# First expert layer: when the rows scattered to DRAM are asked back, what waits behind them, and when they are added

## The reference

```python
y = jnp.zeros((B * S, D), jnp.float32)
for e in range(N_EXPERTS):
    hdn = jax.nn.silu(xt @ w_gate[e]) * (xt @ w_up[e])
    y = y + combine[:, e:e + 1] * (hdn @ w_down[e]).astype(jnp.float32)
...
h = h + g2[:, None, :] * grouped_moe(xn, router_w, router_b, moe_w_gate[layer],
                                     moe_w_up[layer], moe_w_down[layer])
```

## Time and profile before

| | us |
|---|---|
| median of 3 runs | 889.63 (889.59 to 893.86) |
| the profiled execution, its own time | 888.99 |
| its span, first to last instruction | 887.2 |
| PE busy | 844.6 (95%) |
| DVE busy | 329.3 (37%) |
| DMA, mean rate over the span | 358 GB/s |
| stretch of the change: end of layer 0's experts and start of the latent attention | about 469 to 550 |

### The profile page before, as it was taken

The page is one execution under the profiler, slowest core; times in us unless marked ns, Lnnn a source line. Parts: engine busy times, 40 slices in busy tenths (PEclk is TensorE's granted clock), DMA queues, the critical chain, the costliest instruction groups (busy, mean ns, idle before and its releaser), DMA issues.

```text
span 887.2 us, 11840 instructions
## 1 busy us (share of the span) xinstructions
PE 844.6 (95%) x4369; PEld 468.0 (53%) x4369; DVE 329.3 (37%) x598; ACT 177.3 (20%) x354; POOL 161.6 (18%) x271
## 2 busy tenths in 40 slices
PE   6999999999999899999999779999899999999996
PEld 4787444444444555545545347784555555545552
DVE  2826766955302322111112066768511112211114
ACT  2100112121102222122121141250322122122112
POOL 0024000000004522122210131400642212012111
PEclk9999999999999999999999899999999999999999
DMA  8999999998579599999999995579899999979994
GB/s 318 387 321 376 368 366 341 340 382 345 205 271 371 211 406 422 421 422 421 422 422 420 372 400 222 192 293 422 326 360 422 420 421 421 388 312 422 420 404 131
DMA packets 70014, 317.29 MB, mean 358 GB/s; under 512 B 10039, under 2 KB 10170, under 8 KB 44366
## 3 DMA queue, kind: packets, MB, share of 16 engines
q1 hardware_dynamic: 61594, 304.42, 85.6%
q0 software_dynamic: 4976, 8.40, 3.1%
q10 hardware_dynamic: 3396, 3.80, 1.3%
HBM read 311.31 MB, written 15.20 MB: 368 GB/s over the span
## 4 chain that ended last, share of the span: by engine, by line
PE 83%; DMA 6%; SPq 4%; DVE 3%; issue 2%; ACT 1%; ACTq 0%; POOL 0%; DVEq 0%; POOLq 0%
PE bank L730 12%; PE bank L912 11%; PE bank L930 11%; PE bank L899 10%; PE bank L771 6%; PE bank L874 6%; PE bank L671 5%; SPq L470 4%; PE bank L1127 3%; DMA acc<-in_moe_w_up 3%; PE bank L723 2%; DMA part<-outs 1%; PE bank L1081 1%; PE bank L922 1%; PE bank L554 1%
## 5 line engine op out<-in xcount | busy, mean ns | idle before, releaser
L1787 DVE TENSOR_TENSOR arena<-bank,arena 128x256 f32<-128x256 f32 x34 | 21.0, 617 | 254.4 <-PE bank L912 254.4
L1536 DVE SCALAR_TENSOR_TENSOR part<-ring,cpad,part 128x1024 f32<-128x1024 f32 x84 | 111.1, 1323 | 4.1 <-DMA ring<-in_w_mod 1.2
L730 PE MATMUL bank<-ring,xnT 128*128 128x512 f32 x256 | 111.2, 592 | 0.0
L899 PE MATMUL bank<-ring,arena 128*64 128x512 f32 x416 | 92.1, 595 | 0.0
L930 PE MATMUL bank<-ring,arena 128*64 128x512 f32 x352 | 81.7, 606 | 4.4 <-issue 4.4
L912 PE MATMUL bank<-ring,arena 128*64 128x256 f32 x704 | 80.3, 381 | 0.2 <-DMA ring<-in_moe_w_up 0.2
L730 PEld LDWEIGHTS bank<-ring,xnT 128*128 128x128 f32 x256 | 48.4, 190 | 59.4 <-issue 59.3
L874 PEld LDWEIGHTS bank<-arena,y 128*128 128x128 f32 x544 | 64.6, 198 | 15.2 <-issue 15.1
L874 PE MATMUL bank<-arena,y 128*128 128x128 f32 x544 | 67.5, 284 | 1.2 <-DVE arena L1747 1.2
L912 PEld LDWEIGHTS bank<-ring,arena 128*64 128x64 f32 x704 | 50.2, 137 | 30.2 <-issue 8.6
L1315 ACT ACTIVATE arena<-bank,modc,scale 128x128 f32<-128x128 f32 x68 | 25.7, 458 | 180.7 <-PE bank L874 180.7
(11 more groups left out here) (342 smaller groups left out, 1073.0 us busy)
## 6 DMA issues: line engine op xcount, KB each, us to landing
ring<-in_w_mod SPq DMA_DIRECT2D x48, 1024.0 KB, 12.6
ring<-in_moe_w_gate SPq DMA_DIRECT2D x48, 1024.0 KB, 15.4
ring<-in_moe_w_down SPq DMA_DIRECT2D x44, 1024.0 KB, 12.8
ring<-in_moe_w_up SPq DMA_DIRECT2D x40, 1024.0 KB, 12.6
ring<-in_ret_w_in SPq DMA_DIRECT2D x24, 1024.0 KB, 7.3
arena<-in_moe_w_down SPq DMA_DIRECT2D x12, 1024.0 KB, 17.0
arena<-in_moe_w_up SPq DMA_DIRECT2D x12, 1024.0 KB, 16.7
arena<-in_moe_w_gate SPq DMA_DIRECT2D x9, 1024.0 KB, 12.2
```

What stands on the lines that cost most here:

```text
L730: ins = pe.matmul(pair[tt][:], xnT[:, k, tok(tt)], w[:, k, :], start=(k == 0), stop=(k == KT - 1))
L899: ins = pe.matmul(bank[0][e * 64:(e + 1) * 64, :], xgT[:, k, e * 64:(e + 1) * 64], w(e, k), start=(k == 0), stop=(k == KT - 1))
L1536: ins = dve.scalar_tensor_tensor(o, w[:, k, :], c, o, ALU.mult, ALU.add)
```

## The change

It has three parts, all for layer 0 alone. POOL waits, ahead of the two DMAs that bring the rows back, until half 0 of down matrices 46 and 47 is in. SP waits for both of these DMAs to have landed before it issues the first latent weight. DVE adds `part` to `h` behind the two scalings of the last round instead of ahead of them. Layer 1 keeps its order.

```diff
@@ sync
                 if l == 0:
+                    sp.wait_ge(back_in, 32)
                     for j, (kind, n) in enumerate(MLA_ITEMS):
@@ vector, round_of(u, last)
-                    if last:
+                    def returned():
+
                         dve.wait_ge(back_in, 32 * (l + 1))
                         dve.scalar_tensor_tensor(h[:], part[:], first_time[:], h[:], ALU.mult, ALU.add).then_inc(S["h_added"], 1)
                         dve.wait_ge(S["h_added"], u * 6 + 4)
                         dve.memset(first_time[:], 0.0).then_inc(S["h_added"], 1)
+
+                    if last and l:
+                        returned()
                     dve.wait_ge(S["info_ready"], u + 1)
...
                     if last:
+                        if l == 0:
+                            returned()
                         into_h(u)
@@ gpsimd, experts(l)
                 pool.wait_ge(row_none, l + 1)
+                if l == 0:
+                    for m in (6 * PAIRS - 2, 6 * PAIRS - 1):
+                        b, k = HOMES[0][m]
+                        pool.wait_ge(landed[0][b] if b < RING else outside_in[0][b - RING], 16 * k)
                 back = outs[l].rearrange("(t p f) n -> p f t n", p=P, f=2)
```

## The result

The change made the kernel slower: 893.73 us in the median of 13 runs (890.13 to 896.07) beside 890.93 for the kernel before (13 runs); ratio 1.0026, 95% interval 1.0014 to 1.0038, about 2.3 us (the two medians lie 2.8 us apart). The forecast was 887.4, the range ended at 891.4. The three runs shown of before had a median of 889.63, so 1.3 us of the distance are the base; the sign was wrong all the same. The profiled execution took 891.49 us, its span is 889.7.

A forecast was written before the change was run, and what follows sets the result against it. The prediction took PE's waits in layer 0's experts, with rows taking bandwidth from down weights, as the bound. `into_h` 3.5 us earlier, less 1.3 us given back to mod 21, made -2.2 us: median 887.4, range 885.2 to 891.4.

The forecast's parts named there:

- The first PE wait: PE's 4.03 us idle before 494.28, until layer 0's last up weights are in; claimed to stay, with its slow stretch.
- the 4.36 us: PE's idle time before 512.79, until the last half of the down weights lands; claimed to go, with its slow stretch.
- The wait in SP: Step on the latent and mod 20/21 loads issued at 513.1 into an empty queue; claimed 1.3 us given back.
- 2 us of lost flow: Transfer time taken as lost when SP's queue restarts empty at 513.1, moving mod 21's landing from 536.4 to 538.4.
- the head start: 1.28 MB of latent and mod loads already through by 513 in the kernel before; its loss was put at nothing.
- I take 538.4: Forecast landing of mod 21's second half, 536.4 before, with only the 2 us lost.
- the argument on the slowest engine: Claim that the slowest DMA engines, which set a landing, had done next to nothing of the latents at 513.0.
- The prediction's other end, 541.4: Landing of mod 21's second half if all of the 1.28 MB already moved by 513 before is lost.
- the slower rival: Latents and mods start too late, PE waits 4.9 us for mod 21: 890.4, or 892.4 with a slow stretch; chance 0.2.
- PE's clock falls in the new gap: Rival: PE waits 2.8 us for the normalised rows behind its filler and its clock drops: 888.1; chance 0.2.
- The rows come later: Rival: the returned rows land at 515 instead of 513.1, `into_h` starts at 517.6: 889.6, no gain; chance 0.1.
- does not do what it says: Rival: the last down half lands as before because the rows were not what held it: 892; chance 0.03.

The follow-up runs named there:

- sp_only: The kernel before with SP's wait for the returned rows alone added; ratio to before 0.9990.
- mods_first: The changed kernel with SP loading mod 20 and 21 ahead of qa, kvb and qb; ratio to before 0.9973.
- no_move: The changed kernel with the addition of `part` back ahead of the scalings; ratio to before 1.0002.
- warm: The changed kernel with five filler matmuls ahead of PE's waits for mod 21 and the rope products; ratio to before 1.0006.
- mods_early: The changed kernel with SP waiting for the first row DMA alone and loading mod 20 and 21 right behind kva; ratio to before 0.9959.
- early_hold: The changed kernel with a semaphore for each row DMA, SP waiting for the first alone; ratio to before 0.9981.
- early_warm: The changed kernel with SP waiting for the first row DMA alone and five instead of three fillers behind PE's products; ratio to before 0.9972.
- move_only: The kernel before with the addition of `part` moved behind the scalings and nothing else; ratio to before 1.0061.

## Why the prediction was wrong

**Right, to half a us.** The first PE wait stays. The last down half arrives in time, the 4.36 us and the slow stretch behind them go. The rows land at the same time as before. The addition lands on the path and costs 2.5 of the 6 us that PE gains. `into_h` starts at 515.65 (forecast 515.7), kva's loads are issued at 513.2, and PE does not wait for kva. POOL's copy of kva was to stay at 526.55 and came at 528.45, behind the landing of the scatter of no rows; it held PE's rope matmuls (L1006 of before) back by 0.9 us.

**The step that failed** is in "The wait in SP": "I take 2 us of lost flow", with the head start put at nothing, and from it "I take 538.4". It was 542.06, 5.2 us later than before by T, where 2.0 were forecast; sp_only measures the same term by itself: 4.9 us. From SP's release to mod 21 the loads took 28.8 us (513.22 to 542.06), and 27.5 to 28.6 in the five other kernels with a hold and the old order of loads, where the kernel before needed 23.7 from its last down half (512.7 to 536.42).

What the runs show of the reason is the following. The total of the bytes fits: 1.3 MB less up to the release and 0.9 MB less in the 7.3 us behind it make 5.1 us. The flow came back slower than was taken: 229, 310, 351 and 367 GB/s in the four stretches of 2 us from 514 on. But the argument on the slowest engine was not what failed. A load counts its semaphore up 16 times, at times that the trace holds, and it has landed with the last of these counts. In the kernel before, the counts of the last down half came from 502.6 to 512.7, and the last ones of kva's halves followed at 513.8 and 514.8: what was last had indeed done nothing of the latents at 512.7, although kva's first counts came at 508.2. It went on at the full rate, to 536.3 for mod 21 (8.65 MB and ACT's 1.05 MB in 23.6 us are 0.41 MB/us); in the changed kernel the last count came at 542.0. The spread had shrunk from 10.1 us to 3.1 by then (533.2 to 536.3), so whoever was ahead lost most of that lead again. The prediction's other end, 541.4 (541.8 by T), thus had the number, "if all of the head start is lost"; how the 5.2 us divide into head start and restart is not shown and stays open. The row that the choice had to be weighed by (7.37 of 8.65 MB) stood in the text.

**What followed from it** was the slower rival, chance 0.2, "890.4 without that, 892.4 with it": L613 at 548.65, an idle stretch of 5.0 us (forecast for that case 4.9) and the slow clock behind it. Its 892.4 is 2.8 us above the base of then: the distance of the two medians, and 0.5 us more than the ratio gives. Two things have to be kept apart. Why nothing was gained: the late mod 21 took all that `into_h` had won, and mods_first, where it is out of the way, is 4.7 us faster than the changed kernel. Why there was a loss: with the late mod 21 but no slow stretch behind it, no_move and warm are level with before, 2.1 and 1.8 us better than the changed kernel. So nearly all of the 2.3 us are the clock behind PE's wait. From the intervals each of the two differences is uncertain by nearly its own size (an estimate: 1.8 and 1.7 us). What carries the reading is that both agree, and that in both traces the four matmuls took 1.9 to 2.0 us instead of 3.75.

**The rivals.** "PE's clock falls in the new gap" was not what the profile after shows (1.9 us idle, clock 1.00), but mods_first and mods_early show that case, with 1.5 to 2.9 us on kva's matmuls. The Trainium skill (TensorE: Matmul & The Clock Gate, "Why this matters for your kernels") warns against idle gaps between bursts; gaps of 5.0 and 3.6 us here were followed by slow stretches, one of 2.3 us before L615 was not. Near 3 us both are seen: 3.15 us in mods_early was followed by a clock of 0.62, 3.08 us in warm by 1.00. "The rows come later" did not occur, "does not do what it says" neither.

**The chances.** 0.86 on within 0.5% was right by the measure set there; the forecast of a small gain inside it was not. The range ended between the two prices of the slower rival; its upper price, 892.4, and the 1.3 us of the base make the 893.7 that were measured.

## What to carry to other kernels

A transfer held back to protect another can come later by much more than the first idle moments of the queue (here 5.2 us, where 2 were taken): count bytes to the next consumer, and move what is needed first to the front (0.9959 instead of 1.0026 here, with the same hold shortened and the loads reordered). A stage that becomes faster only to wait for a fixed landing can end slower than it was: here four matmuls behind 5.0 us of idle time took 3.75 us at 1.2 GHz instead of 1.88. Ask of each gain what its engine waits for next, and how long.

## What was not expected of the hardware

Releasing the held queue 2.7 us earlier, beside the second row transfer, cost that transfer nothing in early_hold (12.1 us from issue to landing, as in the changed kernel; 13.0 in early_warm) and brought mod 21 forward by 3.8 us, more than the 2.7. Mod 21 came 27.7 us behind the release there and 28.8 in the changed kernel, and no_move, with the late release, had 27.5 as well. So the rest is no more than these kernels differ by, whatever sets it.

Idle stretches of PE did not tell by their length alone what the clock did. In early_hold 2.30 us without matmuls, behind 17 us of unbroken ones, left it at 1.00; in early_warm 2.20 us were followed by 0.61. In move_only PE worked 1.09 of 3.30 us and was at 0.50 in the next 3.3:

```profile
525.70:529.00 3.30, 1.09 (x8) 0.85 (x8) 1.56 (x4) 3.04 (x5) 1.70 (x2) 0.96 1.03 413
529.00:532.30 3.30, 1.97 (x8) 1.57 (x9) 2.47 (x6) 2.09 (x6) 1.45 (x3) 0.50 1.01 405
```

In the changed kernel PE was busy 2.18 of 4.30 us behind its filler and stayed at 1.00.
